# A first weight block in quarters, and experts that gather unscaled rows with a fourth staged weight piece

## What is computed

```python
def _mixer(h, norm_g, w_in, ...):
    u = _rmsnorm(h, norm_g)
    p = u @ w_in                      # gq, gk, gv, dq, dk, dv, gg, and gr, 16 columns wide
    ...
    z = gr.astype(f32) @ gate_w.astype(f32) + gate_b.astype(f32)
...
def _hier_moe(h, norm_g, w_group, b_group, w_expert, b_expert, w_gate, w_up, w_down):
    xf = _rmsnorm(h, norm_g).reshape(t, d)
    ...                               # two of the 32 experts for each token, with a gate each
    def expert_block(args):
        xb, e = args
        hid = jax.nn.silu(xb @ w_gate[e]) * (xb @ w_up[e])
        return hid @ w_down[e]
    ...
    y = jnp.zeros((t, d), out.dtype).at[token_of].add(out)
    return y.reshape(b, s, d).astype(h.dtype)      # added to h by the caller
```

## Time and profile before

| | us |
|---|---|
| median of 3 runs | 1026.22 (1024.59 to 1026.88) |
| the profiled execution | 1026.24 |
| its span in the profile | 1024.5 |
| TensorE busy | 856.6 (84%) |
| VectorE busy | 458.7 (45%) |
| ScalarE busy | 332.9 (32%) |
| GpSimd busy | 23.2 (2%) |

### The profile page before, as it was taken

The page is one execution under the profiler, slowest core; times in us unless marked ns, Lnnn a source line. Parts: engine busy times, 40 slices in busy tenths (PEclk is TensorE's granted clock), DMA queues, the critical chain, the costliest instruction groups (busy, mean ns, idle before and its releaser), DMA issues.

```text
span 1024.5 us, 13523 instructions
## 1 busy us (share of the span) xinstructions
PE 856.6 (84%) x5437; PEld 593.4 (58%) x5437; DVE 458.7 (45%) x859; ACT 332.9 (32%) x534; POOL 23.2 (2%) x35
## 2 busy tenths in 40 slices
PE   8998999999994566767566666656999999999997
PEld 8877888798631131313112131312788899999995
DVE  4778676574621020201102021010876788656695
ACT  5656654764320000000001000000534555455532
POOL 1030010100000000000000000000000000000000
PEclk9999999999998897878869788888999999999999
DMA  9743466587999999999999999999555354444541
GB/s 324 263 165 104 154 230 234 177 335 267 357 402 423 420 422 421 422 421 420 423 421 422 422 421 420 422 421 404 186 189 180 124 165 133 156 151 138 185 143 44
DMA packets 76287, 295.29 MB, mean 288 GB/s; under 512 B 6754, under 2 KB 7236, under 8 KB 53828
## 3 DMA queue, kind: packets, MB, share of 16 engines
q1 hardware_dynamic: 73876, 291.37, 73.9%
q10 hardware_dynamic: 2352, 3.10, 0.9%
HBM read 293.40 MB, written 1.05 MB: 287 GB/s over the span
## 4 chain that ended last, share of the span: by engine, by line
PE 58%; DMA 17%; SPq 14%; DVE 6%; ACT 2%; issue 2%; POOL 0%; POOLq 0%; ACTq 0%; DVEq 0%
DMA ring<-in_w_e_down 16%; PE bank L2448 12%; SPq L644 11%; PE bank L2450 11%; PE bank L2449 11%; PE bank L2894 4%; PE bank L2875 3%; PE bank L2850 3%; SPq L659 2%; PE bank L2382 2%; PE bank L2926 2%; DVE ring_rounded L1445 2%; ACT ring_rounded L907 1%; DMA ring<-in_w_in 1%; PE bank L2979 1%
## 5 line engine op out<-in xcount | busy, mean ns | idle before, releaser
L1445 DVE TENSOR_TENSOR ring_rounded<-ring,ring_rounded 128x2048 fp32r<-128x2048 f32 x79 | 181.0, 2291 | 120.4 <-ACT ring_rounded L907 120.0
L907 ACT ACTIVATE ring_rounded<-ring 128x2048 fp32r<-128x2048 f32 x79 | 151.3, 1915 | 170.3 <-PE bank L2450 157.1
L2875 PE MATMUL bank<-ring,main 128*32 128x512 f32 x768 | 116.6, 762 | 75.1 <-DMA ring<-in_w_e_up 53.4
L2449 PE MATMUL bank<-ring_rounded 128*128 128x256 f32 (+1 forms) x456 | 143.5, 315 | 0.0
L2450 PE MATMUL bank<-ring_rounded 128*128 128x512 f32 x320 | 124.9, 390 | 0.0
L2875 PEld LDWEIGHTS bank<-ring,main 128*32 128x32 f32 x768 | 28.3, 135 | 154.2 <-issue 87.5
L2025 DVE TENSOR_TENSOR h<-bank,h 128x512 f32<-128x512 f32 x32 | 22.0, 690 | 166.0 <-PE bank L2926 166.0
L2894 PE MATMUL bank<-ring,main 128*32 128x512 f32 x384 | 61.0, 789 | 39.9 <-DMA ring<-in_w_e_down 39.2
L2448 PE MATMUL bank<-uT_rounded,ring_rounded 128*128 128x256 f32 x320 | 92.7, 290 | 0.0
L2450 PE MATMUL bank<-uT_rounded,ring_rounded 128*128 128x256 f32 x320 | 90.5, 283 | 0.0
L2449 PEld LDWEIGHTS bank<-ring_rounded 128*128 128x128 f32 x456 | 86.9, 191 | 5.0
(11 more groups left out here) (334 smaller groups left out, 1333.8 us busy)
## 6 DMA issues: line engine op xcount, KB each, us to landing
ring<-in_w_in SPq DMA_DIRECT2D x46, 1024.0 KB, 5.1
ring<-in_w_e_gate SPq DMA_DIRECT2D x44, 1024.0 KB, 25.9
ring<-in_w_e_up SPq DMA_DIRECT2D x44, 1024.0 KB, 26.2
ring<-in_w_e_down SPq DMA_DIRECT2D x36, 1024.0 KB, 25.9
main<-in_w_e_down SPq DMA_DIRECT2D x13, 1024.0 KB, 26.6
main<-in_w_e_up SPq DMA_DIRECT2D x12, 1024.0 KB, 26.9
main<-in_w_e_gate SPq DMA_DIRECT2D x12, 1024.0 KB, 26.4
ring<-in_w_ckv SPq DMA_DIRECT2D x8, 1024.0 KB, 5.0
```

The lines of the kernel that those rows point to most:

```text
L907: a.activation(rounded(hi_half(name, h)), raw_half(name, h), ACT.Copy).then_inc(hi_made, 1)
L1445: v.tensor_tensor(rounded(raw), raw, as_f32(hi_half(name, h)), ALU.subtract).then_inc(split_made, 1)
L2449: mm(dst, left[0], right[1], start=False, stop=False, skip_group_check=True)
L2875: last = mm(bank[2 + part][on, :], xg3[:, h * (KC // 2) + k, on], weight_unit(unit_buffer(p, u), e, KC)[:, k, :], start=h + k == 0, stop=h ...
```

## The change

It has four parts.

1. The first block is loaded and rounded in quarters of 512 KB, between the two halves of xT. TensorE's three products come in another order, with the high by high product in two steps by quarters, and the row factors stand before the last 16 matmuls of half 1. The fillers are 5 and 10. The low-rank weights are laid out by the host (`w_gr`), so that their transfer is packed.
2. SP issues dq's first half before mem, and dq's second half after the parameters; ScalarE squares mem's rows after the decay's Ln.
3. The experts gather from `h` itself. The row norm's factor goes into the selection matrix (`select_slots`), the gains into the drains of the gathered banks (`gathered_low`, `gathered_high`). The outputs of the quads are summed in `normed`, except those of the last two, which are added to `h` directly, with `normed` added once to `h` between.
4. A fourth staged piece goes into `normed`, at an earlier place in SP's order, together with the second half of the piece in `wide_gain`. The two L728 transfers are gone.

```diff
@@ load order
             for j in range(2):
                 at = slice(j * 1024, (j + 1) * 1024)
                 sp.dma_start(lo_a[:, at], A["xT"][:, at]).then_inc(xT_landed[j], 16)
-            load_dense("gqk")
+                for q in range(2):
+                    landed = (first_landed[j], raw_landed[j])[q]
+                    part = 4 * j + 2 * q
+                    sp.dma_start(quarter(raw_half("gqk", j), q).rearrange("p (k n) -> p k n", k=2),
+                                 SOURCE["gqk"][:, part:part + 2, :]).then_inc(landed, 16)
...
             load_dense("gv")
+            load_dense("dq", [0])
             sp.dma_start(token_tiles(mix), token_major(A["mem"][0])).then_inc(mem_landed, 16)
...
+            load_dense("dq", [1])
             sp.dma_start(lo_b, A["memT"]).then_inc(memT_landed, 16)
...
                     load_unit(2, (2,), up_w_of, 0, at=2)
+                    load_staged(3)
+                    load_staged(2, [1])
                     sp.wait_ge(head_summed, len(HEAD_SQUARES))
                     load_staged(0)
...
-                        sp.wait_ge(normed_ready, 2 * SCALED_ROWS.index("h2") + 2)
-                        load_staged(2, [1])
             load_staged(1)
-            for k, used in enumerate((moe.first_used, moe.unit_used)):
-                sp.wait_ge(used, 1)
-                sp.dma_start(weight_unit(0, GROUP - 1, FC)[:, k:k + 1, :], down_w_of[GROUP - 1, :, k:k + 1, :])\
-                    .then_inc(unit_landed[0], 16)
@@ ScalarE
-            split_hi("gqk", [0])
-            split_hi("gqk", [1])
+                for q in range(2):
+                    act.wait_ge((first_landed[j], raw_landed[j])[q], 16)
+                    a.activation(rounded(quarter(hi_half("gqk", j), q)), quarter(raw_half("gqk", j), q), ACT.Copy)\
+                        .then_inc(first_hi, 1)
...
-                a.activation(xgT[:, 0:512], bank[0][:, :], ACT.Copy).then_inc(S.lo_drained, 1)
+                for k in range(KC // 2):
+                    ins = a.activation(xgT[:, k * P:(k + 1) * P], bank[0][:, k * P:(k + 1) * P], ACT.Copy,
+                                       scale=expert_gain[:, k:k + 1])
+                ins.then_inc(S.lo_drained, 1)
...
-                for i, parts_ in ((0, 2), (2, 2), (1, 1)):
+                for i, parts_ in ((0, 2), (2, 2), (3, 1), (1, 1)):
@@ VectorE
-            raw_lo("x", lo_a, uT_flat, "norm_mix")
-            split_lo("gqk", [0])
+            raw_lo("x", lo_a, uT_flat, "norm_mix", (0, 1))
+            split_first(0)
+            raw_lo("x", lo_a, uT_flat, "norm_mix", (2, 3))
...
-            norm_tokens(0)
             split_lo("xv2", [1])
-            norm_tokens(1)
...
-                        last = v.tensor_scalar(select[:, lo:lo + CAP], slot_no[:, :], rank_flat[:, col], None,
-                                               ALU.is_equal)
+                        last = v.tensor_scalar(select[:, lo:lo + CAP], slot_no[:, :], rank_flat[:, col],
+                                               rstd[:, row0 + t:row0 + t + 1], ALU.is_equal, ALU.mult)
...
-            for p in range(2):
-                gathered_high(moe, last_quad + p)
-                dve_quad(moe, last_quad + p, None if p else QUADS - 1,
-                         (lambda: split_lo("iq", [0])) if p else None)
+            gathered_high(moe, last_quad)
+            dve_quad(moe, last_quad, QUADS - 1, "rows")
+            gathered_high(moe, last_quad + 1)
+            dve.wait_ge(moe.added, last_quad * 4 + 8)
+            for t in range(TT):
+                ins = v.tensor_tensor(h[:, t, :], normed[:, t, :], h[:, t, :], ALU.add)
+            link(ins)
+            dve_quad(moe, last_quad + 1, None, "rows", lambda: split_lo("iq", [0]))
@@ TensorE
-            keep_busy(wait_free("xrow0"), 9)
+            keep_busy(wait_free("xrow0"), 5)
...
-            keep_busy(wait_free("xrow0"), 20)
+            keep_busy(wait_free("xrow0"), 10)
...
-                for part, (x_part, w_part) in enumerate(((0, 0), (0, 1), (1, 0))):
+                for x_part, w_part, chunks in ((0, 0, (0, 1)), (0, 0, (2, 3)), (1, 0, range(4)), (0, 1, range(4))):
...
+                    elif w_part:
+                        pe.wait_ge(first_split, 2 * h_ + 2)
+                        if h_:
+                            row_factors(["xrow0", "xrow1"], x_spread, 1)
...
-                        last = mm(dst, normed[:, t, k * P:(k + 1) * P], sel3[:, t, :], start=t == 0,
-                                  stop=t == TT - 1)
+                        last = mm(dst, h[:, t, :].rearrange("p (q c) -> p c q", c=KC)[:, k, :], sel3[:, t, :],
+                                  start=t == 0, stop=t == TT - 1)
```

More of the change, by code:

```diff
@@ L377, in build @@
         staged = [[main[:, 5376:6400], squares[:, :]], [mem2T[:, 0:1024], mem2T[:, 1024:2048]],
-                  [y_slots, wide_gain[:, :]]]
+                  [y_slots, wide_gain[:, :]], [normed[:, 0, :], normed[:, 1, :]]]
         score = c.take(384)
@@ L409, in build @@
         gates_split = sem("low_rank_weights_split")
+        first_landed = [sem(f"first_block_half{h}_landed_in_part") for h in range(2)]
+        first_hi, first_split = sem("first_block_quarters_hi_made"), sem("first_block_quarters_split")
         hi_moved, y_split = sem("input_hi_moved"), sem("branch_inputs_split")
@@ L444, in build @@
         moe = ExpertSems(sem, "moe")
-        staged_landed = [sem(f"staged_piece_landed{i}") for i in range(3)]
+        staged_landed = [sem(f"staged_piece_landed{i}") for i in range(GROUP)]
         last_landed = [sem(f"last_unit_chunk_landed{k}") for k in range(3)]
@@ L967, in _ @@
             a.activation(k_dec, k_dec, ACT.Ln, bias=1.0).then_inc(gla_act, 1)
+            act.wait_ge(mem_landed, 16)
+            square_rows("mem", mix.rearrange("p (t d) -> p t d", t=TT),
+                        memT.rearrange("p (t d) -> p t d", t=TT))
             split_hi("dq", [1])
@@ L1467, in _, with raw_lo @@
             wait_drained(dve, "cols")
-            def raw_lo(prefix, raw, hi, gain):
-                for c2 in range(4):
+            def raw_lo(prefix, raw, hi, gain, chunks=range(4)):
+                for c2 in chunks:
                     in_order(dve, hi_moved, HI_BANKS, f"{prefix}T{c2}")
@@ L1498, in two_chunks, with split_first @@
                 return x.rearrange("p (c t) -> p c t", c=2)
-            raw_lo("x", lo_a, uT_flat, "norm_mix")
-            split_lo("gqk", [0])
+            def split_first(h):
+                for q in range(2):
+                    dve.wait_ge(first_hi, 2 * h + q + 1)
+                    raw = quarter(raw_half("gqk", h), q)
+                    v.tensor_tensor(rounded(raw), raw, as_f32(quarter(hi_half("gqk", h), q)), ALU.subtract)\
+                        .then_inc(first_split, 1)
+            raw_lo("x", lo_a, uT_flat, "norm_mix", (0, 1))
+            split_first(0)
+            raw_lo("x", lo_a, uT_flat, "norm_mix", (2, 3))
             dve.wait_ge(gates_landed, 16 * 2)
@@ L1509, in _ @@
             link(v.tensor_tensor(qk_gain[:, 2:4], cols[:, q0:q0 + 2], cols[:, k0:k0 + 2], ALU.mult))
-            split_lo("gqk", [1])
+            split_first(1)
             row_mean("x")
@@ L2023, in add_outputs @@
                         b = bank[(6, 2)[t] + half]
-                        hs = h[:, t, half * 512:half * 512 + 512]
-                        v.tensor_tensor(hs, b[:, :], hs, ALU.add).then_inc(S.added, 1)
+                        at = slice(half * 512, half * 512 + 512)
+                        if into == "new sums":
+                            ins = v.tensor_copy(normed[:, t, at], b[:, :])
+                        else:
+                            to = (normed if into == "sums" else h)[:, t, at]
+                            ins = v.tensor_tensor(to, b[:, :], to, ALU.add)
+                        ins.then_inc(S.added, 1)
             def shift_ranks(S, n, i):
@@ L2031, in shift_ranks, with dve_quad @@
                 v.tensor_scalar(at, at, -float(CAP), None, ALU.add).then_inc(S.ranks_shifted, 1)
-            def dve_quad(S, n, following, between=None):
+            def dve_quad(S, n, following, into="sums", between=None):
                 dve.wait_ge(S.gathered, n + 1)
@@ L2042, in dve_quad @@
                 hidden(S, n)
-                add_outputs(S, n, between)
+                add_outputs(S, n, into, between)
             select_slots(moe, 0)
@@ L2050, in _ @@
             mark(moe.added, 4)
-            with dve.Fori(0, 2 * LAST_PAIR) as i:
+            gathered_high(moe, 0)
+            dve_quad(moe, 0, 1, "new sums")
+            with dve.Fori(1, 2 * LAST_PAIR) as i:
                 gathered_high(moe, i)
```

73 lines of the change are left out of this document (37 added, 36 removed).

## The result

The changed kernel takes 1031.46 us (median of 5 runs, 1030.99 to 1032.16), the kernel before 1026.85 in the same session (1024.59 to 1027.62). The ratio is 1.0048, with a 95% interval of 1.0037 to 1.0059. The forecast was 1024.5, range 1022.2 to 1026.6: wrong in sign. The profiled execution, the slowest of the five, has a span of 1030.4 us, 5.9 more than before.

The account below looks back on a forecast made before the run. TensorE bounds the first and last stages, the stream of the experts' weights the middle one. Terms -0.96 + 0.2 - 0.94 = -1.7 us, from 1026.24, gave 1024.5 us, range 1022.2 to 1026.6.

Parts of the forecast that it names:

- term 1: First block: gv starts at 27.65 in place of 28.61, and all behind it shifts by -0.96 us.
- term 2: First gather: reading h with a step of eight numbers costs +0.2 us, between 0 and +1.1.
- term 3: Ahead of the eight expert loads: weight pieces issued earlier give -0.94 us; at least 0, at most -3.7.
- the masks' chain: Between row factors and gv: copy, scaling, four mask casts and gv's low part take 6.5 us, untouched by the edit.
- The other 3 us: Before gv: of some 4 us TensorE by itself would gain, the part that becomes a wait for VectorE.
- rival B: Start: with fewer fillers TensorE stays cold, first matmuls 1.3 us late, gain before gv gone; 1025.5; chance 0.17.
- rival D: Gather: loads slowed by the step; at twice the spacing it costs 3.7 us, 1028.1; chance 0.12.
- The dry queue before L742: Ahead of the eight expert loads: the DMA queue runs dry from about 277 to 280.5 us.
- dq's rounding behind the squares of mem: Block dq: second half's rounding and low part stay hidden with 0.3 us to spare; uncovered, up to 2.1 late.
- rival C: Block dq: the squares of mem or a late dq are not hidden; 1 us back, 1025.5; chance 0.08.
- the gate as the place that sets the end: Experts' stream: its end follows when the eight loads leave (278.5), not all bytes; iq's release near 716.1.
- the last quad's extra pass: Last quad: an added pass over h and the sums, about 2.4 us, where VectorE idles 10.11 us; no cost.

Follow-up runs that it names:

- e5: The changed kernel with its four lambda loads taken from ScalarE's queue and issued by SyncE behind block gv: 1030.79 us, ratio 1.0048.
- e8: The changed kernel with its gather's eight column groups read at steps of 4, 8, 16 and 32 B, two groups each: 1028.08 us (one run).
- e10: The changed kernel with the 1.5 MB of weight pieces it moved forward issued where they were before: 1030.71 us, ratio 1.0045.
- e9: The changed kernel with eight filler calls on TensorE between the low-rank gates' last product and block gv: 1028.90 us, ratio 1.0030.
- e3: The changed kernel with its gather loading 128 neighbouring columns of h instead of every eighth one: 1027.04 us, ratio 1.0010.
- e1: The kernel before with the first-block part of the change alone, including dq's load and squares of mem moved: 1028.60 us, ratio 1.0028.
- e7: The kernel before with only the packed load of the low-rank gate weights added: 1026.87 us, ratio 1.0009.
- e12: The kernel before with the first-block part, lambda loads behind gv, and row factors and gv's low part sooner; gather still packed: 1021.97 us, ratio 0.9964.
- e6: The changed kernel with the low-rank gate weights loaded as before, in 1024 pieces of 64 bytes: 1031.44 us, ratio 1.0062.
- e4: The changed kernel with the low part of gv's first half made between VectorE's second and third mask casts: 1028.95 us, ratio 1.0026.
- e2: The changed kernel with the first block as before, except the packed load of the low-rank gate weights: 1030.16 us, ratio 1.0040.

## Why the prediction was wrong

At iq's release the forecast was -1.7 us and the profiles show +5.6. Of the 7.3 between them, 4.4 lie in term 1 (-0.96 forecast, +3.44 found) and 3.7 in term 2 (+0.2, +3.93); term 3 gives 0.8 back. Each of the two terms alone turns the sign.

**Term 1, the first half of it.** "A quarter of the weights costs half of 1.92, so 1.0: the first matmuls start near 8.6, the second quarter's near 9.6" was the step that lost the gain. The first came at 8.86, the second at 10.58: I let the second quarter follow at ScalarE's pace, but it was still on its way, and ScalarE waited for it until 9.37. So TensorE reaches the row factors at 22.06 by its own work (e5) and not at 21.0, and the masks' chain of 6.5 us, which I had right, gives 28.61: nothing gained.

**Term 1, the late rows.** The prediction did not ask when x's rows land. The packed load brought the lambda broadcasts forward, the DMA rate fell to 162 GB/s, and in the changed kernel's profile the row factors came another 0.66 later (22.72). It varies: in e8 and e10, with the same start, gv began at 28.58 and 28.70, and by the ratios moving the broadcasts away gained nothing (e5).

**Term 1, the wait.** "The other 3 us turn into a wait of TensorE before gv" was right (2.98), but I priced the wait at nothing. In the changed kernel's profile it cost 2.6 us of gv at half clock, in the others 1.5 to 2.8; e9, without the fall, is 1.9 us faster by the ratio. I had looked for a cold TensorE (rival B) at the fillers, where it did not matter, and not at the idle stretch that my own sum produced. (At the fillers rival B's sign did show: they took 421 ns until 6.8, where I had forecast 275 from 6.3 on. But they ended at 8.63, and TensorE waited for ScalarE until 8.86, so it cost nothing.) Term 1 was to be -0.96 and is +3.44 in this profile; the gather starts at 271.92 in e3 and 271.24 in e8 with the same start, so it is +1.5 to +3.4, and +2.9 by e1's ratio.

**Term 2.** I took +0.2 from the turning of the hidden rows, whose spacing at a step of 16 B is the gather's own 0.117. It is +3.93: rival D, at twice the spacing. The spacing could not be carried over, only the slowing of the load. The packed loads of the turning take 142 ns, those with a step 209, so 1.47 times; for the gather's 192 ns that would be some 280. If the 90 ns more of each load show in full, 32 of them cost some 2.8 us, an estimate, beyond my upper bound of 1.1, though still under what came (335 ns). The Trainium skill, page Advanced Engine Details and Errata, section Memory Cachelines, says that two accesses to a 16 byte line are needed for full speed; by that rule a step of 8 B is fast and one of 16 B slow, and e8 agrees (197 and 330 ns). I had set the rule aside because "the trace doesn't agree"; but the row I went by had the slower load in it, 209 ns against 142.

**Term 3.** Forecast -0.94, behind the gate, as the first landing was to come after 3.66 in place of 4.6. It came after 4.0 (3.9 in e3), so the mechanism is there, at 0.6 to 0.7. Gate to release shortened by 1.75 in the profiles of before and changed, by 0.96 between e1 and e3, and by only 0.13 from e7 to the changed kernel, so these profiles don't confirm the size, and where 0.96 meets the forecast that may be luck. In the changed kernel itself the moved bytes did nothing (e10), because the gather's delay had emptied the queue already; the two terms do not add.

**What held.** The dry queue before L742; the drains and the selection of the first gather at no cost (e3's 9.59); dq's rounding behind the squares of mem, at 44.19 with TensorE not waiting (against rival C); the gate as the place that sets the end.

The sum as measured in the profiles: +3.44 + 3.93 - 1.75 = +5.6 at iq's release, where the span shows +5.9 and the medians +4.6. The missing 0.3 lies behind the release: from there to the end it is 306.6 to 306.7 us in the four profiles with the old experts (before, e1, e7, e12) and 306.9 to 307.6 in the ten with the changed ones. Which of their edits costs it was not tried, so the "no cost" of the last quad's extra pass is not confirmed. The profiled execution is 0.7 us above its median, and the terms hold for it alone.

## What to carry to other kernels

When an edit makes an engine finish earlier ahead of an unchanged chain, price the new idle stretch as well: look up what TensorE's granted clock does after a gap of that length, and fill the gap or shorten the chain. Before a weight load gets a step, compare the duration of a load with and without one, not the spacing in a place where something else hides it. And when a small load is made cheaper, ask which transfers behind it in its queue now run earlier, and what they run beside.

## What was not expected of the hardware

- Weight loads of 128 x 128 fp32 for a matmul: 192 ns packed, 197 at a step of 8 B, 330 at 16 B, 335 at 32 B. In a transpose a load with a step of 16 B takes only 209 ns (142 packed). Why the same step costs 67 ns there and 138 in the gather was not tried.
- Four broadcast loads of 32 KB each go with a fall of the DMA rate from some 400 to 162 GB/s for 2 us in the changed kernel (ScalarE's queue) and to 174 in e5 (SP's queue). In the kernel before and in e6, where they follow the scattered load of 1024 pieces, the rate fell only to 277 and 298 GB/s (16 to 18 us). What in them does it stays open.
- After 2.98 us of idling TensorE's granted clock fell from 1.00 to 0.50, in the changed kernel, e1 and e5 from gv's first matmul, in e3, e6, e8 and e10 up to five matmuls later, and stayed low for seven to thirteen intervals of 0.43 us. It also fell in e4 (1.23 us of idling, 3.6 us of work, 1.53 of idling) and at gqk in e2 (2.78). It did not in e9 (1.00) and e7 (1.11).
- The four issues behind the low-rank load on ScalarE's queue took up to 1.55 us each in e6 (1024 pieces of 64 B) and up to 0.68 in the changed kernel (packed). The pieces alone don't explain it: the kernel before has them too and took up to 0.91, and e2, packed, took up to 1.00.
